# Two transformer blocks on one core: the norms of four heads at once, products of two heads in turns, stage boundaries reordered, and constant products on TensorE

## The reference

```python
h = rms_norm(x, norm1_w); proj = h @ w_in          # block 1: q, k, v, z, xbc, dt
q = rms_norm(q.reshape(b, s, 8, 128), q_norm_w)    # a norm over the 128 columns of each of 8 heads
k = rms_norm(k.reshape(b, s, 8, 128), k_norm_w)
attn = causal softmax attention(q, k, v)           # one block of 256 keys
y = Mamba-2 scan(silu(conv(xbc)), softplus(dt)); y = rms_norm(y * silu(z), ssm_norm_w)
x = x + concat(attn, y) @ w_out
u = causal_dwconv(rms_norm(x, norm2_w) @ w_up)     # the FFN, width 5632
x = x + (silu(u_gate) * u_val) @ w_down
shift, scale, gate = split(silu(c) @ w_ada + b_ada)  # block 2
h = rms_norm(x, g) * (1 + scale) + shift
proj = h @ w_in_2                                  # dilated attention and retention
x = rms_norm(x + gate * (concat(...) @ w_out_2), final_gain)
```

## Time and profile before

| | |
|---|---|
| median of three executions | 1561.35 us |
| the three | 1561.07, 1561.35, 1567.77 us |
| the profiled execution, its time | 1567.55 us |
| its span (first to last instruction) | 1565.9 us |
| TensorE busy | 1542.4 us, 13186 matmul records |
| VectorE, ScalarE, GpSimd busy | 1156.0, 787.9, 29.7 us |
| mean granted clock of TensorE | 0.994 |

### The profile page before, as it was taken

The page is one execution under the profiler, slowest core; times in us unless marked ns, Lnnn a source line. Parts: engine busy times, 40 slices in busy tenths (PEclk is TensorE's granted clock), DMA queues, the critical chain, the costliest instruction groups (busy, mean ns, idle before and its releaser), DMA issues. The chain is left out here.

```text
span 1565.9 us, 33333 instructions
## 1 busy us (share of the span) xinstructions
PE 1542.4 (99%) x13186; PEld 1524.3 (97%) x13186; DVE 1156.0 (74%) x1370; ACT 787.9 (50%) x960; POOL 29.7 (2%) x56
## 2 busy tenths in 40 slices
PE   9999998999999999999999999999899999999997
PEld 8999997999999999999999999999899999999997
DVE  7777798658898878888788887888854644764754
ACT  7545545645554444444444444444554644454543
POOL 0000000000000000000000000000000000000000
PEclk9999999999999999999999999999999999999999
DMA  9474555448787767677676776765365554445441
GB/s 339 157 269 162 194 170 176 161 164 279 259 294 268 270 235 286 234 261 270 233 287 232 264 269 233 289 231 200 133 242 189 189 186 151 161 158 181 162 159 71
DMA packets 85361, 339.31 MB, mean 217 GB/s; under 512 B 9488, under 2 KB 9760, under 8 KB 78752
## 3 DMA queue, kind: packets, MB, share of 16 engines
q1 hardware_dynamic: 77328, 281.05, 52.1%
q0 software_dynamic: 7232, 54.55, 9.8%
q10 hardware_dynamic: 720, 2.53, 0.4%
HBM read 335.97 MB, written 2.12 MB: 216 GB/s over the span
## 5 line engine op out<-in xcount | busy, mean ns | idle before, releaser
L1260 PE MATMUL PS<-gh,whi 128*128 128x256 f32 x3504 | 985.6, 281 | 2.9 <-DVE gl L1144 1.7
L1262 PE MATMUL PS<-gl,whi 128*128 128x256 f32 x3504 | 974.2, 278 | 0.0
L1264 PE MATMUL PS<-gh,wlo 128*128 128x256 f32 x3504 | 973.9, 278 | 0.0
L658 DVE TENSOR_TENSOR wlo<-raw,whi 128x1024 fp32r<-128x1024 f32 x528 | 642.7, 1222 | 348.7 <-ACT whi L296 346.2
L296 ACT ACTIVATE whi<-raw 128x1024 fp32r<-128x1024 f32 x528 | 556.5, 1059 | 642.9 <-PE PS L1264 640.1
L1260 PEld LDWEIGHTS PS<-gh,whi 128*128 128x128 f32 x3504 | 660.9, 189 | 8.6 <-issue 5.2
L1262 PEld LDWEIGHTS PS<-gl,whi 128*128 128x128 f32 x3504 | 662.2, 189 | 2.6 <-issue 1.9
L1264 PEld LDWEIGHTS PS<-gh,wlo 128*128 128x128 f32 x3504 | 660.3, 188 | 0.0
L1260 PE MATMUL PS<-ah,whi 128*128 128x256 f32 x688 | 190.1, 276 | 0.9 <-DVE al L1028 0.9
L1264 PE MATMUL PS<-ah,wlo 128*128 128x256 f32 x688 | 189.9, 276 | 0.0
L1262 PE MATMUL PS<-al,whi 128*128 128x256 f32 x688 | 189.9, 276 | 0.0
(11 more groups left out here) (228 smaller groups left out, 787.8 us busy)
## 6 DMA issues: line engine op xcount, KB each, us to landing
raw<-weights SPq DMA_DIRECT2D x528, 512.0 KB, 3.7
ada_w<-w_ada POOLq DMA_DIRECT2D x48, 1024.0 KB, 6.5
EM<-rows POOLq DMA_DIRECT2D x1, 3072.0 KB, 11.8
outT<-X SPq DMA_DIRECT2D x4, 512.0 KB, 3.0
X<-xT SPq DMA_DIRECT2D x3, 512.0 KB, 8.2
c<-const ACTq DMA_DIRECT2D x1, 1536.0 KB, 7.0
c_act<-c_rows POOLq DMA_DIRECT2D x1, 1024.0 KB, 6.5
X<-xT SPq DMA_DIRECT2D x2, 256.0 KB, 4.8
```

Source lines behind the costliest of these rows:

```text
L658: dve.tensor_tensor(wlo[:, j % SPLIT, :], raw[:, j, :], whi[:, j % SPLIT, :].bitcast(F32), ALU.subtract).then_inc(s_lo, 1)
L1260: pe.matmul(out[:, t, :], whi[:, b, w], hi[:, kt, :], start=first and half == 0 and (apart or t % 2 == 0), stop=False, skip_group_check=True)
L1262: pe.matmul(out[:, t, :], whi[:, b, w], lo[:, kt, :], start=False, stop=False, skip_group_check=True)
L1264: mm = pe.matmul(out[:, t, :], wlo[:, b, w], hi[:, kt, :], start=False, stop=last and half == 1, skip_group_check=True)
```

## The change

The norms run for four heads at once, in slots 62 and 74. The squares of four heads' q and k are summed by four matmuls with 32 columns of ones each, head h into partitions 32h to 32h+31 of one bank, so that one root and one reciprocal (128 x 512) serve four heads. The factor of q is not multiplied into q any more: two transposes bring it into columns, and it becomes the per-partition factor in the step that adds the mask, which is cut in two. The factor of k is spread over the partitions by four matmuls with a repeated column of the identity, and VectorE multiplies k by it and by the product of both gains. In the slots of attention the transposes come first, and the scores of one head and the weighted sum of another take turns, half by half; the weighted sum's halves swap places.

The first norm's sum and root move from slot 6 to 7, the steps of dt are pulled together, and silu of c moves from slot 78 to 67. At the boundary the table load of the root moves ahead, `last_add(3)` comes before the folding, the column sums take tiles 1 to 3 first, and the first unit of in2 multiplies the parts with gh before it waits for gl. `idle(n)` issues n products of the identity with a constant, 256 columns, whose result nobody reads: two behind the column sums, two in the first FFN round on TensorE (which is taken out of the loop), two in slot 2 of in2. In out2 the final gains are spread over twelve slots, and two squares come one slot later. The end multiplies and writes in seven pieces in place of four.

The diff, cut to its core:

```diff
-NORMS = (58, 61, 64, 67, 74, 75, 76, 77)
+NORMS = (62, 74)
...
+GAINS = (15, 17, 18, 19, 20, 21, 22, 23, 25, 26, 27, 28)
+FINAL = ((4, 1), (5, 1), (6, 2), (8, 2), (10, 2))
...
+        qk_norm = small[:, 272:273]
+        def q_col(h, c):
+            return small[:, 256 + 8 * (h // 4) + 4 * c + h % 4:257 + 8 * (h // 4) + 4 * c + h % 4]
...
-            for q, signal, count in ((1, s_fin, 1), (2, s_fin, 2), (0, s_pool, 1), (3, s_fin, 4)):
-                sp.wait_ge(signal, count)
-                sp.dma_start(outT[:, 4 * q:4 * q + 4, :], X[:, 4 * q:4 * q + 4, :]).then_inc(s_out, 16)
-            sp.wait_ge(s_out, 64)
+            for n, (first, tiles) in enumerate(FINAL):
+                sp.wait_ge(s_fin, n + 1)
+                sp.dma_start(outT[:, first:first + tiles, :], X[:, first:first + tiles, :]).then_inc(s_out, 16)
+            sp.wait_ge(s_pool, 1)
+            sp.dma_start(outT[:, 0:4, :], X[:, 0:4, :]).then_inc(s_out, 16)
+            sp.wait_ge(s_fin, len(FINAL) + 2)
+            sp.dma_start(outT[:, 12:16, :], X[:, 12:16, :]).then_inc(s_out, 16)
+            sp.wait_ge(s_out, 16 * (len(FINAL) + 2))
...
+                if k == 3 and c == 2:
+                    act.activation(small[:, 241:242], col("eps"), ACT.Sqrt).then_inc(s_warm, 1)
...
-                    if t == 0:
-                        act.activation(small[:, 241:242], col("eps"), ACT.Sqrt).then_inc(s_warm, 1)
...
+            def head_squares(b, k):
+                if b == 0:
+                    act.wait_ge(s_y, SSM_HEADS // 2)
+                else:
+                    act.wait_ge(s_nr, b)
+                act.wait_ge(s_evac, (G_IN + 9 if b else G_IN + 7) + 2)
+                first = (Q1 if b else Q0) + 4 * k
+                act.activation(HSQ[:, :, k, :], QKVZ[:, first:first + 4, :], ACT.Square).then_inc(s_nsq, 1)
+            def head_root(b):
+                act.wait_ge(s_nr, b + 1)
+                if b:
+                    act.wait_ge(s_kb, b)
+                act.activation(HRT[:, :, :], PS[:, 7, :].rearrange("p (c d) -> p c d", c=2), ACT.Sqrt,
                                bias=col("eps"), scale=1.0 / P).then_inc(s_nrt, 1)
...
-                if n == 78:
+                if n == 67:
...
+                for b in range(2):
+                    if n - NORMS[b] in (-2, -1):
+                        head_squares(b, n - NORMS[b] + 2)
+                    if n == NORMS[b]:
+                        head_root(b)
...
+                if d == 2:
+                    act.activation(small[:, 241:242], col("eps"), ACT.Sqrt).then_inc(s_warm, 1)
+                if d < 3:
...
-                if s in (13, 15, 23, 31):
-                    c = (13, 15, 23, 31).index(s)
+                if s in (14, 16, 24, 31):
+                    c = (14, 16, 24, 31).index(s)
                     if c < 3:
                         act.wait_ge(s_evac, G_OUT2 + c + 3)
                     squares(3, c, SQX4)
-                    if c < 3:
-                        for t in range(4 * c, 4 * c + 4):
-                            gained(t, SQUARES[3] + c + 1)
+                if s in GAINS:
+                    t = GAINS.index(s)
+                    gained(t, SQUARES[3] + t // 4 + 1)
...
-                if n == 15:
+                if n == 14:
...
-                if n == 17:
+                if n == 16:
...
-                if n == 18:
+                if n == 16:
...
+            def head_inverse(b):
+                dve.wait_ge(s_nrt, b + 1)
+                dve.reciprocal(HRT[:, :, :], HRT[:, :, :]).then_inc(s_inv, 1)
+            def q_factors(b):
+                dve.wait_ge(s_rq, b + 1)
+                if b == 0:
+                    dve.tensor_tensor(qk_norm, col("q_norm"), col("k_norm"), ALU.mult).then_inc(s_rqc, 1)
+                rows = PS[:, 7, 0:S].rearrange("p (c h r) -> p c h r", c=2, h=4)[:, :, :, 0]
+                dve.tensor_scalar(small[:, 256 + 8 * b:264 + 8 * b].rearrange("p (c h) -> p c h", c=2), rows, SCALE, None,
+                                  ALU.mult).then_inc(s_rqc, 1)
+            def k_norm(h):
+                dve.wait_ge(s_kb, h // 4 + 1)
+                dve.wait_ge(s_rqc, 1)
+                t = QKVZ[:, head_tile(K0, K1, h), :]
+                dve.scalar_tensor_tensor(t, t, qk_norm, PS[:, 5 + h % 4 // 2, S * (h % 2):S * (h % 2) + S],
+                                         ALU.mult, ALU.mult).then_inc(s_qk, 1)
...
-                        dve.scalar_tensor_tensor(SB[:, h % 2, :, :].rearrange("p c d -> p (c d)")[:, 0:3 * P],
-                                                 PS[:, 4, 0:3 * P], SCALE, mask[:, :], ALU.mult, ALU.add).then_inc(s_sb, 1)
+                        dve.wait_ge(s_rqc, 2 + h // 4)
+                        for c, at in enumerate((slice(0, P), slice(P, 3 * P))):
+                            ins = dve.scalar_tensor_tensor(seen(h, c), PS[:, 4, at], q_col(h, c), mask[:, at],
+                                                           ALU.mult, ALU.add)
+                        ins.then_inc(s_sb, 1)
...
+                if n in (58, 59):
+                    ssm_norm(n - 58)
+                for b in range(2):
+                    if n == NORMS[b] + 1:
+                        head_inverse(b)
+                    if n == NORMS[b] + 3:
+                        q_factors(b)
+                    if n - NORMS[b] in (3, 4):
+                        for h in range(2):
+                            k_norm(4 * b + 2 * (n - NORMS[b] - 3) + h)
...
-                    if i is last and j == 6:
-                        ffn_lo(i, ah2, al2)
                     if j % 2:
                         add_to_x(unit + (16 + j), grp + (2 + j // 2), (G_FF + j // 2) % 2, 4 * (j // 2))
+                    if i is last and j == 5:
+                        ffn_lo(i, ah2, al2)
...
             last_add(2)
+            last_add(3)
             dve.wait_ge(s_fold, 3)
             dve.tensor_tensor(SQX2[:, 0, 0, :], SQX2[:, 0, 0, :], SQX2[:, 1, 0, :], ALU.add).then_inc(s_near, 1)
             near(2, 0, SQX2, 1)
-            last_add(3)
...
+                if s in (16, 24):
+                    sum_chunk(3, (16, 24).index(s) + 1, SQX4)
...
-            for first, tiles in ((4, 4), (8, 4), (12, 3)):
+            for first, tiles in FINAL + ((12, 3),):
...
+            def product_high_first(out, need):
+                for kt in range(2):
+                    pe.wait_ge(s_gh, 2 * DT + 6 + kt + 1)
+                    for w, x in ((whi, gh), (wlo, gh), (whi, gl)):
+                        if x is gl:
+                            pe.wait_ge(s_gl, need(kt))
+                        for t in range(4):
+                            at = 512 * kt + P * t
+                            mm = pe.matmul(out[:, t, :], w[:, 0, at:at + P], x[:, kt, :],
+                                           start=kt == 0 and w is whi and x is gh and t % 2 == 0, stop=False,
+                                           skip_group_check=True)
                 mm.then_inc(s_used, 1)
...
+                order = (1, 2, 3, None) if k == 2 else (None, 2, 3)
+                for n, t in enumerate(order):
+                    if t is None:
+                        src = buf[:, 0, 0, :]
+                        pe.wait_ge(s_near, 2 * (k - 1))
+                    else:
+                        src = near_tile(k, t)
+                        pe.wait_ge(s_sq, SQUARES[k] + 4 + t)
...
+                if k == 2:
+                    idle(2)
+            def idle(n):
+                for _ in range(n):
+                    pe.matmul(PS[:, 4, 0:S], ident, cst[:, 0:S], start=True, stop=True)
...
+                if blk == B_IN2 and n == 0:
+                    product_high_first(acc_tiles(grp % 2), need)
+                    return
...
+            def weighted(h, layer, PTS, VS, parts):
+                H = layer * HEADS + h
+                for b in parts:
...
+                    mm = pe.matmul(PS[:, 6, first:S], VS[:, h % 2, b, :], PTS[:, h % 2, b, 0:S - first],
+                                   start=(b == 1), stop=(b == 0), skip_group_check=True)
...
+            def first_heads(n):
+                def head(step):
+                    h, odd = divmod(n - ATT0 - step, 2)
+                    return h if not odd and 0 <= h < HEADS else None
+                new, mid, old = head(0), head(4), head(6)
+                if mid is not None:
+                    attention(4, mid, 0)
+                for part in range(2):
+                    if new is not None:
+                        scores(new, 0, QKVZ[:, head_tile(Q0, Q1, new), :], QKVZ[:, head_tile(K0, K1, new), :], (part,))
+                    if old is not None:
+                        weighted(old, 0, PTS1, VS1, (1 - part,))
...
+                if n == 57:
+                    for g in range(2):
+                        pe.wait_ge(s_yf, g + 1)
+                        pe.matmul(PS[:, 6 + g, 0:S], ones, SQY[g][:, 0, :], start=True, stop=True).then_inc(s_ysum, 1)
+                for b in range(2):
```

(118 more changed lines are left out.)

60 lines of the change are left out of this document (11 added, 49 removed).

## The result

The changed kernel took 1572.84, 1577.58, 1577.60 and 1578.15 us, median 1577.6, against 1561.2 for the kernel before beside it: ratio 1.0099, 95% interval 1.0078 to 1.0120. It is 1.0% slower, where 0.8% faster was forecast.

The account below looks back on a forecast made before the run. TensorE, busy 1542.4 of 1565.9 us, was taken as the bound, through waits and a long unit spacing. The terms summed to -18.9 against 1567.55, giving 1548.6 us (chance 0.52), own range 1545 to 1552.

Parts of the forecast that it names:

- rival 2: FFN's unit stream falls into the long spacing, 640 us becoming 664: +24, 1573 us; chance 0.07.
- Start: First norm's sum one slot later and dt steps in time remove waits of 0.4 and 0.7: -1.1 us.
- Column groups: Sums of the heads: four 512-column products on column groups overlap, about 1.1 us, where in turn they take 3.4.
- rival 3: Sums of the heads: the column-group products go in turn, +4.6 us, 1553; chance 0.04.
- New waits: At the first heads TensorE waits for the new norm chain: 1.5 us in the first batch, 0.3 in the second.
- The stall: At the first heads, 262 to 274 us: all 7.9 us lost to idling, half clock and refilling goes, -7.9.
- Rival 5: The stall of 5.4 us at the heads moves to the reciprocals' results and in2 stays long: 1561; chance 0.07.
- The boundary: Boundary and in2's first eight units: VectorE starts on `gl` earlier, eighth unit ends 2.6 us sooner; -0.9 at 1.2 GHz.
- in2: in2 after its first eight units turns from long to short spacing: -5.9 us, bounds 0 and -5.9.
- rival 1: in2 stays in long spacing, 5.9 us above the forecast: 1554.5 us; chance 0.22.
- Rival 4: A stall remains at the heads or boundary with the lower clock behind it: +3 to +6 us, 1553; chance 0.08.
- The end: Final multiplies and writes in seven pieces: first starts 0.8 us earlier, pieces end 0.5 later; -0.3.

## Why the prediction was wrong

The step that failed is in the FFN's part: "A pair of constant products, +0.9, with nothing to hide them, since TensorE is full there." The pair itself took 471.94 - 470.84 - 0.23 = 0.87. What it does to the 5566 matmuls behind it, +24.9, was left out of the sum. The prediction had it as rival 2, with its mechanism, place and price (+24, 1573), and gave it 0.07. Three readings led there. The single products that it looked at all left the stream short, and it let the pair count as two of them; here the number decides. And of in2 it wrote "What two of them do after a long spacing no row shows", but didn't ask the same of a short one. Last, it argued from four executions of the kernel before, which has no such pair in it, so their closeness said nothing of what a pair does. With the 24.9 in its sum it gives 1573.5; the profiled execution took 1572.84.

The other steps, against the traces (differences of the same unit's time before and after):

- *Start*, -1.1: the two waits went (-0.6, -1.0), a third grew by 0.3, to the 0.6 at L1530. Right.
- *Column groups*: four products 512 wide took 1.20, forecast 1.1. Timeline of the changed kernel around both halves of the first batch:

```profile
203.22 0.28 PE L1303 MATMUL PS<-gh,wlo 128*128 128x256 f32 x1
203.43 1.06 PE L1577 MATMUL PS<-HSQ,cst 128*32 128x512 f32 x8
204.43 0.39 PE L1299 MATMUL PS<-gh,whi 128*128 128x256 f32 x1
204.65 0.28 PE L1301 MATMUL PS<-gl,whi 128*128 128x256 f32 x1
...
212.59 0.28 PE L1303 MATMUL PS<-gh,wlo 128*128 128x256 f32 x1
214.29 0.44 PE L1583 MATMUL PS<-cst,HRT 128*128 128x128 f32 x2 [1.43 <-DVE HRT L876]
214.57 1.89 PE L1588 MATMUL PS<-HRT,cst 128*128 128x256 f32 x8
216.11 0.47 PE L1299 MATMUL PS<-gh,whi 128*128 128x256 f32 x1
216.41 0.28 PE L1301 MATMUL PS<-gl,whi 128*128 128x256 f32 x1
```

  204.65 - 203.22 - 0.23 = 1.20, where four in turn would take 3.4: rival 3 is out. The Trainium skill (TensorE: Matmul & The Clock Gate, Part 3) says that weight loads overlap running matmuls only when the row group differs. The trace disagrees: each of the four loads uses all rows, and the starts of their first matmuls lie at 203.43 to 203.45. The prediction's reading, that by the skill the groups would go nearly in turn, also went further than the Trainium skill does: its table in the same part lists 2.38 times the speed for three column tiles of 512 columns. The rest takes 216.41 - 212.59 - 0.23 = 3.6, forecast 0.3 + 1.7 + 1.5.
- *New waits*, 1.5 and 0.3: 1.43 and 0.30.
- *The stall*, -7.9: -8.15, with no wait at the scores. Rival 5 is out.
- *`ffn_lo`*, -0.9 and 0.16 of refilling: -1.2.
- *The boundary*, -2.6: from unit 380 to 391 it took 39.9 before and 37.2 after, -2.8. But over the 17 traces of the changed kernel and its versions it took 37.2 to 39.2, and it goes by the granted clock: 37.2 in the three where this stayed at 1.00, 37.3 to 38.2 in the ten where it averaged 0.86 over the 12 us around its fall, 38.4 to 39.2 in the four where it averaged 0.72. The prediction had bounds of this kind, -0.9 with a fall to 1.2 GHz and -2.6 without; against the kernel before it is -0.7 at the least and -2.8 at the most. Rival 4's lower clock behind the boundary is thus there in 14 of 17 traces, at up to 2.0 us, though not in the one against which the sum is checked.
- *in2*, -5.9: so in the profiled execution, and a coin's throw elsewhere. Of 68 executions with the FFN short, 33 lay in the lower band; of the kernel before's 74, 58. So rival 1 deserved as much as the forecast. What differs in in2 between the two kernels is the small waits for `gl` at its first units; that these are the whole reason is argued, not shown.
- *out2*, -0.8 and -0.9: together -2.2, from unit 454 to the last.
- *The end*, -0.3: from the last unit on it took 11.4 before and 11.7 after, +0.3. In 13 of the 17 traces of the changed kernel and its versions it took 11.0 to 11.2, as forecast, and in four, this one among them, 11.7 to 11.9. What differs starts ahead of the first piece: in the four the granted clock fell to 0.50 within 2.8 us of the last unit, in the thirteen 3.3 us or more behind it, and the eight spreading products that the first multiply waits for took 1.80 in place of 1.16. The changed kernel and the one with three products:

```profile
1561.95 1.80 PE L1368 MATMUL PS<-cst,small 128*128 128x128 f32 x8 [0.55 <-DVE small L722]
```

```profile
1537.09 1.16 PE L1368 MATMUL PS<-cst,small 128*128 128x128 f32 x8 [0.55 <-DVE small L722]
```

Like against like, both profiled with in2 long and no pair in the FFN: 1553.29 - 1567.55 = -14.3, forecast -18.9 + 5.9 - 0.9 = -13.9.

## What to carry to other kernels

Where TensorE is busy all the time, compare records per microsecond of the long stretches first: 4% lay in a spacing that shows neither as a wait nor in the clock. An insertion has two prices there, its own time and what it does to the stream behind it; read the second from the same insertion in the same number, and where no row has it, give it weight in proportion to the length of the stream behind. Run a kernel often enough to see its bands, and compare like bands: the same program gave 1547 and 1554.

## What the runs showed of the hardware

- A stream of products of 128 x 256 with a weight load each runs at clock 1.00 in one of two steady spacings, 113.3 and 117.8 ns, and keeps it, over 5566 matmuls in one trace, until something interrupts it.
- Insertions of full-width float32 products on constants, among units at clock 1.00: two turned short to long 12 times of 12 (four: 1 of 1) and left long long 3 times of 3; one left short short 6 times of 6 and long long 3 times of 3; three kept each, once and twice. The first norm's sum, a single one too, turned long to short 5 times of 5, and short to long once, behind a wait of 0.41, so the rule for one product has exceptions.
- Interruptions as small as 0.04 us behind the regular start, and waits up to 0.9, turned the spacing in either direction or in none. What inside TensorE sets it was not found.
- Four float32 products with 32 columns of weights and 512 moving columns, on four column groups and all 128 rows, took 1.20 us together, where one of full width takes 0.86.
